# Differential attention on one NeuronCore: scores kept in SBUF by the maximum's pass and issued a step ahead, meta parts of four units turned beside the values' sums

## The chip, the cores and the metric

The kernel runs on one core of one Trainium2 chip. A core has five engines that run side by side, each through its own list of instructions in order, and that wait for one another by semaphores: TensorE (PE; its weight loads are listed apart as PEld), VectorE (DVE), ScalarE (ACT), GpSimd (POOL) and SyncE (SP, which only issues transfers here). The metric is the device time of one execution, in microseconds (us), as the median of several runs.

## The reference

The reference is one layer of an encoder over 1024 tokens and 16 learned meta tokens (width 1024): a projection, windowed attention (8 heads), differential attention (8 heads), an output projection, and a mixture of 32 experts, 4 for each token. What matters here is differential attention:

```python
scale = DIFF_DQ ** -0.5                       # DIFF_DQ = 32, DIFF_H = 8, DIFF_DV = 64
def one_block(qs):                            # 128 query rows at a time
    a, b = qs
    p1 = softmax(einsum('bqhd,bkhd->bhqk', a, k1) * scale)   # over 1024 + 16 keys
    p2 = softmax(einsum('bqhd,bkhd->bhqk', b, k2) * scale)
    return einsum('bhqk,bkhd->bqhd', (p1 - lam * p2), v)
```

So each head has two score matrices over the same keys, two softmaxes, and one product with the values. The head's output is normalised afterwards, per head, in the stage that follows.

## The kernel before

The kernel is a chain of stages, each a block of instructions for all engines with a barrier behind it: `project`, `attend_window`, `attend_diff`, `route` (output projection and routing), `experts`, `combine`. Only `attend_diff` is touched.

`attend_diff` goes through U = 64 units, a unit being one head h and one tile t of 128 query rows (unit n = 8h + t). Each engine's list is written out by hand over steps n = 0 to 71, a step doing different parts of several units:

- TensorE: `scores(n, i)` for i = 0, 1 gives the scores of half i of unit n, 128 rows by 1024 keys, into PSUM `s_ps[i]` (two banks, one buffer for each half). It waits until ScalarE has used the scores of the same half of unit n-1 (`s_used`). The queries' scores with the 16 meta keys are made for a whole head at once (`meta_scores`, 16 small products into `x_ps`). The combined weights of a unit are turned by eight transposes into `t_ps` (`transpose_part`, two groups of four) and a ninth, of the 16 meta columns, into `x_ps` (`transpose_meta`). `values` sums the product of values and turned weights for four units together (512 columns) in `o_ps[0:64]`: nine products, eight of 128 keys and one of the 16 meta keys. Two of the nine are issued in a step, in each fourth step three: one by itself between `scores(n, 0)` and the transposes, two after `scores(n, 1)`. Last, the sum of a group of four units is turned back by four small transposes into `x_ps` (L792).
- VectorE: `maximum(n, i)` is a `tensor_reduce` over the 1024 scores in PSUM (L640) and a 1-column minimum with the meta keys' part (L647). Then `invert` (reciprocal of the sums), `copy_meta` (the turned meta part, PSUM to SBUF, each unit), `combine_halves` (e0 + ratio x e1, 1040 columns, L662), and in some steps `store_out` (four scalings of 64 columns, L677) and `meta_scores` (two operations, each eighth step).
- ScalarE: for each half an exponential of the 1024 scores from PSUM (L600) and one of the 16 meta scores (L602), each followed by the read of its sum; between the two halves the two copies of the turned weights of unit n-2 (L587); in each fourth step the copy of the values' sum (L612).
- GpSimd: the sum of the two partial sums (L707) and the ratio (L711).

The order of the work in TensorE's list within step n is: `scores(n, 0)`, [one value product in each fourth step], the transposes of unit n-2, `scores(n, 1)`, two value products, [turning back], [`meta_scores`]. SP's list in this stage: the next stage's weights first, then the queries and keys of head h once all scores of head h-2 are made.

Of the kernel before, what the change touches and what calls it, by code (L numbers as in the profile page):

```python
# [22 lines left out]
ALU = mybir.AluOpType  # L23
ACT = mybir.ActivationFunctionType
AX = mybir.AxisListType
# [489 lines left out]
def attend_diff(nc, a, v_all, mixed, qk_dram, stacks, weights):  # L515
# [3 lines left out]
    with ExitStack() as ctx:  # L519
# [5 lines left out]
        e = sb("e", [P, 2, 2, KEYS])  # L525
        dsb = sb("dsb", [P, 2, KEYS])
# [3 lines left out]
        meta_s = sb("meta_s", [P, 2, 2 * NT, N_META])  # L530
        meta_nm = sb("meta_nm", [P, 2, 2 * NT])
        seq_nm = sb("seq_nm", [P, 4])
        nm = sb("nm", [P, 4])
        ls = sb("ls", [P, 2, 2, 2])
# [10 lines left out]
        scores_ready, max_ready, exp_done = sem("scores_ready"), sem("max_ready"), sem("exp_done")  # L545
        nm_ready, s_used = sem("nm_ready"), sem("scores_used")
        inverted = sem("inverted")
        total_done, ratio_done, combined = sem("total_done"), sem("ratio_done"), sem("combined")
        t_ready, t_copied = sem("p_transposed"), sem("pt_copied")
        x_ready, x_copied, meta_max = sem("x_ready"), sem("x_copied"), sem("meta_max")  # L550
        o_ready, ot_done = sem("o_ready"), sem("ot_copied")
        dve_chain = sem("dve_chain2")
# [3 lines left out]
        STEPS = U + 8  # L556
        block = ctx.enter_context(nc.Block())


        copied_in = lambda n: (n - 9) // 4 if n >= 9 and (n - 9) % 4 == 0 and (n - 9) // 4 < NG else None  # L560
        back_in = lambda n: copied_in(n - 1)

        order = [("scores", 0)]
        for n in range(STEPS):
            if 2 <= n <= U + 1:
                order.append(("meta", n - 2))
            if back_in(n) is not None:
                order.append(("back", back_in(n)))
            if n % NT == NT - 1 and n + 1 < U:
                order.append(("scores", (n + 1) // NT))  # L570
# [10 lines left out]
        def _(act):  # L581
            def copy_part(u, g):

                act.wait_ge(t_ready, 2 * u + g + 1)
                if g == 0 and u % 4 == 0 and u >= 8:
                    act.wait_ge(o_ready, u // 4 - 1)
                act.copy(pt[:, (u // 4) % 2, 4 * g:4 * g + 4, (u % 4) * P:(u % 4 + 1) * P],  # L587
                         t_ps[:, g, :].rearrange("p (c n) -> p c n", n=P)).then_inc(t_copied, 1)
# [3 lines left out]
            for n in range(STEPS):  # L592
                for i in range(2):
                    if n < U:
                        act.wait_ge(nm_ready, 2 * n + i + 1)
                        if n >= 2 and i == 0:
                            act.wait_ge(combined, n - 1)
                            act.wait_ge(total_done, n - 1)
                        k = (2 * n + i) % 4
                        act.activation(e[:, n % 2, i, 0:SEQ], S(i), ACT.Exp, bias=nm[:, k:k + 1],  # L600
                                       accum_out=ls[:, n % 2, 0, i:i + 1]).then_inc(s_used, 1)
                        act.activation(e[:, n % 2, i, SEQ:KEYS], meta_s[:, (n // NT) % 2, 2 * (n % NT) + i, :], ACT.Exp,  # L602
                                       bias=nm[:, k:k + 1], accum_out=ls[:, n % 2, 1, i:i + 1]).then_inc(exp_done, 1)
                    if i == 0 and 2 <= n <= U + 1:
                        copy_part(n - 2, 0)
                        copy_part(n - 2, 1)
                g = copied_in(n)
                if g is not None:
# [3 lines left out]
                    act.copy(ot[:, :], o_ps[0:DV, :]).then_inc(ot_done, 1)  # L612

        @block.vector
        def _(dve):
# [11 lines left out]
            def meta_scores(h):  # L627
                dve.wait_ge(x_ready, use_of[("scores", h)] + 1)
                if h >= 2:
                    dve.wait_ge(exp_done, 2 * NT * (h - 1))  # L630
# [1415 lines left out]
```

## Time and profile before

| | us |
|---|---|
| median of 3 runs (lowest to highest) | 2760.18 (2759.84 to 2764.11) |
| the profiled execution, its own time | 2772.98 |
| span of the profile | 2771.0 |
| `attend_diff` in it, from its first product to the next stage's first transfer | 478.5 to 820.7 |
| TensorE busy over the span | 2447.0 (88%) |
| VectorE busy | 1766.8 (64%) |
| ScalarE busy | 1435.9 (52%) |
| granted TensorE clock, mean over the span | 0.938 |

Times inside the profile are counted in us from the start of its span. The granted clock is a share of full speed, which is 2.4 GHz; the other level is 1.2 GHz. A group of instructions is named by its line of the kernel. An fp32 or fp32r product is recorded as several MATMUL rows: a value product is two of them, a half unit's scores two. Ends of matmuls are modelled; starts are not.

### The profile page before, as it was taken

How to read it: one execution, taken by the hardware profiler on the slowest of the kernel's cores; microseconds unless marked ns; L12 is line 12 of the kernel's file. 1: busy time of each engine (PE TensorE's matmuls, PEld its weight loads, DVE VectorE, ACT ScalarE, POOL GpSimd, SP SyncE). 2: the span in 40 equal slices, each digit the busy share in tenths (PEclk: the TensorE clock that was granted, in tenths of full speed). 3: DMA queues.
4: the chain of work that ended last, by engine and by line, in shares of the span. 5: the costliest groups of instructions: out<-in, count | busy, mean ns of one | idle time of the engine just before them, and what ended most of it. 6: DMA issues, size and time to landing. Idle time of an engine off the chain costs nothing. (4 is left out here: it accounts for less than half of the span.)

```text
span 2771.0 us, 33947 instructions
## 1 busy us (share of the span) xinstructions
PE 2447.0 (88%) x10437; PEld 1703.2 (61%) x10438; DVE 1766.8 (64%) x2143; ACT 1435.9 (52%) x1863; POOL 472.0 (17%) x539
## 2 busy tenths in 40 slices
PE   7999599899989928999999998999999999999950
PEld 3555265444435516777778776777777777777740
DVE  1444355899964446767675566666776667688654
ACT  1111154777751126675664565655665657577540
POOL 1443200111101221121211122111211111112110
PEclk9999799899999959999999999999999999999975
DMA  4221450232103347787785677776876669699767
GB/s 182 65 65 51 108 108 23 84 62 62 31 20 77 83 163 273 261 283 289 266 319 203 218 265 278 243 253 211 292 259 243 223 231 340 223 351 337 247 241 276
DMA packets 248412, 540.75 MB, mean 195 GB/s; under 512 B 27200, under 2 KB 58176, under 8 KB 246224
## 3 DMA queue, kind: packets, MB, share of 16 engines
q1 hardware_dynamic: 226304, 501.10, 53.8%
q0 software_dynamic: 20880, 34.49, 3.4%
q10 hardware_dynamic: 1152, 4.19, 0.4%
q8 instruction: 42, 0.69, 0.1%
q14 instruction: 34, 0.28, 0.0%
HBM read 513.63 MB, written 60.15 MB: 207 GB/s over the span
## 5 line engine op out<-in xcount | busy, mean ns | idle before, releaser
L1661 DVE TENSOR_TENSOR wlo<-raw,whi 128x2048 fp32r<-128x2048 f32 x387 | 881.6, 2291 | 360.6 <-ACT whi L1546 359.4
L1546 ACT CAST whi<-raw 128x2048 fp32r<-128x2048 f32 x387 | 737.5, 1913 | 275.7 <-PE gl_ps L1816 149.3
L1818 PE MATMUL gl_ps<-whi,xt_hi 128*128 128x512 f32 x1056 | 428.7, 406 | 64.1 <-ACTq L1609 40.9
L1819 PE MATMUL gl_ps<-wlo,xt_hi 128*128 128x512 f32 x1056 | 421.7, 399 | 0.0
L1820 PE MATMUL gl_ps<-whi,xt_lo 128*128 128x512 f32 x1056 | 420.1, 398 | 0.0
L1818 PEld LDWEIGHTS gl_ps<-whi,xt_hi 128*128 128x128 f32 x1056 | 204.5, 194 | 117.2 <-issue 68.7
L422 PE MATMUL pp<-w_in_sb,ut 128*128 128x512 f32 (+3 forms) x688 | 271.2, 552 | 0.8 <-issue 0.8
L1820 PEld LDWEIGHTS gl_ps<-whi,xt_lo 128*128 128x128 f32 x1056 | 204.4, 194 | 44.5
L1819 PEld LDWEIGHTS gl_ps<-wlo,xt_hi 128*128 128x128 f32 x1056 | 204.9, 194 | 41.8
L1482 POOL CAST sel<-onehot 128x128 fp32r (+1 forms) x66 | 48.2, 731 | 1017.6 <-PE gl_ps L1824 774.9
L1818 PE MATMUL y_ps<-whi,ht_hi 128*128 128x512 f32 x512 | 208.3, 407 | 0.0
L422 PEld LDWEIGHTS pp<-w_in_sb,ut 128*128 128x128 f32 (+1 forms) x688 | 125.4, 185 | 130.1 <-issue 125.0
L1820 PE MATMUL y_ps<-whi,ht_lo 128*128 128x512 f32 x512 | 202.0, 395 | 0.0
L1819 PE MATMUL y_ps<-wlo,ht_hi 128*128 128x512 f32 x512 | 201.7, 394 | 0.0
L600 ACT ACTIVATE e<-s_ps,nm 128x1024 f32<-128x1024 f32 x128 | 143.5, 1121 | 72.9 <-DVE nm L647 72.9
L1816 PE MATMUL gl_ps<-wlo,xt_hi 128*64 128x512 f32 x416 | 164.5, 395 | 0.0
L1815 PE MATMUL gl_ps<-whi,xt_hi 128*128 128x512 f32 x416 | 162.2, 390 | 0.0
L640 DVE TENSOR_REDUCE seq_nm<-s_ps 128x1 f32<-128x1024 f32 x128 | 155.7, 1217 | 9.6 <-PE s_ps L721 7.1
L763 PE MATMUL o_ps<-pt,v_all 128*64 128x512 f32 (+1 forms) x288 | 142.9, 611 | 0.8 <-ACT ot L612 0.8
L1477 POOL DMA_INDIRECT xg<-v_dram,idn x66 | 116.2, 1760 | 146.8 <-DMA idn<-slot_dram 115.3
L247 ACT COPY pr<-pp 128x512 f32<-128x512 f32 (+3 forms) x43 | 23.0, 540 | 185.5 <-PE pp L422 185.5
L1293 PE MATMUL o_ps<-w_out_sb,mt 128*128 128x512 f32 x256 | 116.7, 606 | 0.9 <-DVE mt L1173 0.9
(260 smaller groups left out, 3532.6 us busy)
## 6 DMA issues: line engine op xcount, KB each, us to landing
raw<-in_w_mlp SPq DMA_DIRECT2D x390, 1024.0 KB, 5.1
yk<-y_dram SPq DMA_DIRECT2D x8, 2048.0 KB, 7.8
w_in_sb<-in_w_in SPq DMA_DIRECT2D x8, 1152.0 KB, 14.2
k_st<-qk_dram SPq DMA_DIRECT2D x32, 260.0 KB, 7.5
xs<-in_x SPq DMA_DIRECT2D x16, 512.0 KB, 7.3
q_st<-qk_dram SPq DMA_DIRECT2D x32, 256.0 KB, 6.6
qk_dram<-qk_hi SPq DMA_DIRECT2D x8, 832.0 KB, 4.5
qk_dram<-qk_lo SPq DMA_DIRECT2D x8, 832.0 KB, 7.5
```

Of the source, the lines that this page charges most:

```text
L422: ins = pe.matmul(pp[0:r, n % 4, 0:c1 - c0], ut[:, t % 2, k, 0:r], w_sb[:, k, c0:c1], start=(k == 0), stop=(k == KC - 1))
L600: act.activation(e[:, n % 2, i, 0:SEQ], S(i), ACT.Exp, bias=nm[:, k:k + 1], accum_out=ls[:, n % 2, 0, i:i + 1]).then_inc(s_used, 1)
L640: dve.tensor_reduce(seq_nm[:, k:k + 1], S(i), AX.X, ALU.max, negate=True).then_inc(max_ready, 1)
L763: ins = pe.matmul(o_ps[0:DV, :], vt, pt[0:r, g % 2, c, :], start=(c == 0), stop=(c == 8))
L1293: ins = pe.matmul(o_ps[:, 2 * (t % 2) + b, :], mt[:, t % 2, k, :], w_sb[:, k, 512 * b:512 * b + 512], start=(k == 0), stop=(k == KC - 1))
L1546: act.copy(whi[:, k % SPL, :], raw[:, k % RAW, :]).then_inc(hi_done, 1)
L1661: dve.tensor_tensor(wlo[:, k % SPL, :], raw[:, k % RAW, :], whi[:, k % SPL, :].bitcast(F32), ALU.subtract).then_inc(lo_done, 1)
L1815: ins = pe.matmul(bank, xh[:, 1, kc, :], hi, start=start, stop=stop, skip_group_check=True)
L1816: ins = pe.matmul(bank[0:FEW], xh[:, 1, kc, 0:FEW], lo, start=False, stop=stop, skip_group_check=True)
L1818: pe.matmul(bank, xh[:, half, kc, :], hi, start=start, stop=False, skip_group_check=True)
L1819: pe.matmul(bank, xh[:, half, kc, :], lo, start=False, stop=False, skip_group_check=True)
L1820: return pe.matmul(bank, xl[:, half, kc, :], hi, start=False, stop=stop, skip_group_check=True)
```

## The change

Eight parts, all inside `attend_diff`:

1. The maximum's pass becomes a `tensor_tensor_reduce` that adds a tile of zeros to the scores, multiplies by -1, writes the negated scores (1024 columns) into `e` in SBUF, and takes the minimum, starting from the meta part. The separate 1-column minimum and its buffers go.
2. GpSimd places the 16 negated meta scores of both halves behind them in `e`; ScalarE then does one exponential in place over 1040 columns of SBUF (scale -1), whose sum goes straight to `total`. GpSimd's addition of partial sums goes.
3. `scores(n + 1, i)` is issued in step n and waits for the maximum's pass over unit n, half i (`nm_ready`) instead of ScalarE's exponential.
4. The turned meta part goes to `o_ps[0:16]`, four units side by side, while the values' sum goes to `o_ps[64:128]` of the same bank; ScalarE copies it once for four units (`copy_meta`), VectorE's copy for each unit goes.
5. The value products start a step later (LAG = 7) and stand at the head of TensorE's step; the ninth is issued in one row with two others.
6. ScalarE's copies of the turned weights are split around the second exponential.
7. `back`, `store_out` and `meta_scores` move to the front of the step, on VectorE in between `invert` and the second maximum; the meta scores of the next head are made two steps earlier.
8. STEPS is U + 9 instead of U + 8.

```diff
@@ scalar
+            def exponent(n, i):
+                act.wait_ge(nm_ready, 2 * n + i + 1)
+                act.wait_ge(meta_in, n + 1)
+                if n >= 16 and i == 0:
+                    act.wait_ge(ratio_done, n - 15)
+                k = (2 * n + i) % 4
+                act.activation(e[:, n % 2, i, :], e[:, n % 2, i, :], ACT.Exp, bias=nm[:, k:k + 1], scale=-1.0,
+                               accum_out=total[:, n % 16, i:i + 1]).then_inc(exp_done, 1)
+            def copy_meta(g):
+                act.wait_ge(m_ready, 4 * g + 4)
+                if g >= 2:
+                    act.wait_ge(o_ready, g - 1)
+                act.copy(pt[0:N_META, g % 2, 8, :], o_ps[0:N_META, :]).then_inc(m_copied, 1)
...
             for n in range(STEPS):
+                if n < U:
+                    exponent(n, 0)
+                g = weighed_in(n)
                 if g is not None:
                     act.wait_ge(o_ready, g + 1)
...
+                    act.copy(ot[:, :], o_ps[DV:P, :]).then_inc(ot_done, 1)
+                if 2 <= n <= U + 1:
+                    copy_first(n - 2)
+                if n < U:
+                    exponent(n, 1)
+                if 2 <= n <= U + 1:
+                    copy_second(n - 2)
+                    if (n - 2) % 4 == 3:
+                        copy_meta((n - 2) // 4)
@@ vector
             def maximum(n, i):
-                dve.tensor_reduce(seq_nm[:, k:k + 1], S(i), AX.X, ALU.max, negate=True).then_inc(max_ready, 1)
...
-                dve.tensor_tensor(nm[:, k:k + 1], seq_nm[:, k:k + 1], meta_nm[:, (n // NT) % 2, at:at + 1],
-                                  ALU.min).then_inc(nm_ready, 1)
...
+                    dve.wait_ge(exp_done, 2 * n + i - 3)
+                    dve.wait_ge(combined, n - 1)
+                dve.tensor_tensor_reduce(e[:, n % 2, i, 0:SEQ], S(i), zero[:, :], -1.0, meta_nm[:, (n // NT) % 2, at:at + 1],
+                                         ALU.add, ALU.min, nm[:, k:k + 1]).then_inc(nm_ready, 1)
...
                     maximum(n, 0)
                 if 1 <= n <= U:
                     invert(n - 1)
+                if back_in(n) is not None:
+                    store_out(back_in(n))
+                if scores_in(n) is not None:
+                    meta_scores(scores_in(n))
                 if n < U:
                     maximum(n, 1)
                 if 1 <= n <= U:
                     combine_halves(n - 1)
@@ gpsimd
+            for n in range(U + 1):
+                if n < U:
+                    h, at = n // NT, 2 * (n % NT)
+                    if n >= 2:
+                        pool.wait_ge(combined, n - 1)
+                    pool.wait_ge(x_copied, use_of[("scores", h)] + 1)
+                    pool.tensor_copy(e[:, n % 2, :, SEQ:KEYS], meta_s[:, h % 2, at:at + 2, :]).then_inc(meta_in, 1)
+                if n >= 1:
...
@@ tensor
             def scores(n, i):
...
-                    pe.wait_ge(s_used, 2 * n + i - 1)
+                    pe.wait_ge(nm_ready, 2 * n + i - 1)
...
+                pe.transpose(o_ps[0:N_META, (u % 4) * P:(u % 4 + 1) * P], dsb[:, u % 2, SEQ:KEYS], ident[:, :]
+                             ).then_inc(m_ready, 1)
...
+                    ins = pe.matmul(o_ps[DV:P, :], vt, pt[0:r, g % 2, c, :], start=(c == 0), stop=(c == 8),
+                                    skip_group_check=True)
...
             for n in range(STEPS):
+                if back_in(n) is not None:
+                    back(back_in(n))
+                if scores_in(n) is not None:
+                    meta_scores(scores_in(n))
+                if LAG <= n < U + LAG:
+                    q, i = divmod(n - LAG, 4)
+                    values(9 * q + 2 * i, 9 * q + 2 * i + (3 if i == 3 else 2))
+                if n + 1 < U:
+                    scores(n + 1, 0)
+                if 2 <= n <= U + 1:
+                    transposes(n - 2)
+                if n + 1 < U:
+                    scores(n + 1, 1)
```

## Rows read from the trace of the kernel before

**Rows 1.** Stretches: us; busy PE, PEld, DVE, ACT, POOL; granted clock; DMA share; GB/s.

```profile
478.40:518.60 40.20, 28.03 (x97) 17.71 (x98) 29.55 (x53) 25.58 (x67) 3.29 (x13) 0.66 0.37 129
...
558.60:798.40 239.80, 229.41 (x993) 112.07 (x991) 217.50 (x399) 190.25 (x494) 25.83 (x97) 1.00 0.21 45
798.40:820.70 22.30, 18.09 (x59) 6.28 (x58) 6.95 (x19) 7.04 (x16) 0.87 (x3) 1.00 0.00 1
```

**Rows 2.** TensorE in order of time, 640 to 702: start, us, what, idle before.

```profile
641.01 1.95 PE L736 MATMUL x_ps<-k_st,q_st 128*128 128x16 f32 x16
...
661.21 0.73 PE L721 MATMUL s_ps<-k_st,q_st 128*128 128x512 f32 x2
662.92 1.09 PE L744 MATMUL t_ps<-ident,dsb 128*128 128x128 f32 x8 [0.98 <-DVE dsb L662]
...
680.77 1.95 PE L736 MATMUL x_ps<-k_st,q_st 128*128 128x16 f32 x16
682.58 0.71 PE L721 MATMUL s_ps<-k_st,q_st 128*128 128x512 f32 x2
683.12 1.03 PE L744 MATMUL t_ps<-ident,dsb 128*128 128x128 f32 x8
...
684.02 0.72 PE L721 MATMUL s_ps<-k_st,q_st 128*128 128x512 f32 x2
684.67 1.93 PE L763 MATMUL o_ps<-pt,v_all 128*64 128x512 f32 x4
686.53 0.73 PE L721 MATMUL s_ps<-k_st,q_st 128*128 128x512 f32 x2
687.20 1.07 PE L763 MATMUL o_ps<-pt,v_all 128*64 128x512 f32 x2
688.20 1.09 PE L744 MATMUL t_ps<-ident,dsb 128*128 128x128 f32 x8
...
689.80 2.07 PE L763 MATMUL o_ps<-pt,v_all 128*64 128x512 f32 x4
691.80 0.73 PE L721 MATMUL s_ps<-k_st,q_st 128*128 128x512 f32 x2
692.83 1.09 PE L744 MATMUL t_ps<-ident,dsb 128*128 128x128 f32 x8 [0.29 <-DVE dsb L662]
...
696.69 0.73 PE L721 MATMUL s_ps<-k_st,q_st 128*128 128x512 f32 x2
697.46 1.09 PE L744 MATMUL t_ps<-ident,dsb 128*128 128x128 f32 x8
```

**Rows 3.** Groups by line in `attend_diff`: count, busy us, mean ns, idle before.

```profile
L640 DVE TENSOR_REDUCE seq_nm<-s_ps 128x1 f32<-128x1024 f32 x128 | 155.7, 1217 | 9.6 <-PE s_ps L721 7.1
L600 ACT ACTIVATE e<-s_ps,nm 128x1024 f32<-128x1024 f32 x128 | 143.5, 1121 | 72.9 <-DVE nm L647 72.9
...
L662 DVE SCALAR_TENSOR_TENSOR dsb<-e,ratio 128x1040 f32<-128x1040 f32 x64 | 83.3, 1302 | 5.3 <-POOL ratio L711 0.5 <-issue 0.4
```

**Rows 4.** The same view of the windowed attention before it, shapes apart.

```profile
L957 DVE CUSTOM_DVE_ANT_0 sm<-sa_ps,masks 128x400 f32<-128x400 f32 x48 | 24.8, 558 | 1.6 <-PE sa_ps L888 1.6
...
L957 DVE CUSTOM_DVE_ANT_0 sm<-sa_ps,masks 128x272 f32<-128x272 f32 x16 | 6.5, 432 | 21.5 <-PE sa_ps L888 21.5
```

**Rows 5.** VectorE in order of time: first half maxima of units 0 and 7.

```profile
482.29 1.23 DVE L640 TENSOR_REDUCE seq_nm<-s_ps 128x1 f32<-128x1024 f32 x1 [0.22 <-PE s_ps L721]
...
518.68 1.23 DVE L640 TENSOR_REDUCE seq_nm<-s_ps 128x1 f32<-128x1024 f32 x1 [0.47 <-PE s_ps L721]
```

**Rows 6.** TensorE in order of time in the same first steps.

```profile
496.18 1.79 PE L744 MATMUL t_ps<-ident,dsb 128*128 128x128 f32 x8 [2.37 <-DVE dsb L662]
...
497.83 2.17 PE L721 MATMUL s_ps<-k_st,q_st 128*128 128x512 f32 x4
```

**Rows 7.** The end of the stage, TensorE in order of time.

```profile
796.09 0.73 PE L721 MATMUL s_ps<-k_st,q_st 128*128 128x512 f32 x2
...
812.09 6.36 PE L763 MATMUL o_ps<-pt,v_all 128*64 128x512 f32 x14
```

More of the change, by code:

```diff
@@ L693, in _ @@
                     combine_halves(n - 1)
-                if back_in(n) is not None:
-                    store_out(back_in(n))
-                if n % NT == NT - 1 and n + 1 < U:
-                    meta_scores((n + 1) // NT)
         @block.gpsimd
@@ L701, in _ @@
             pool.wait_ge(lam_done, 1)
[L702 to L712 removed]
+            for n in range(U + 1):
[6 more added lines that the diff above has]
+                if n >= 1:
+                    u = n - 1
+                    pool.wait_ge(inverted, u + 1)
+                    if u >= 2:
+                        pool.wait_ge(combined, u - 1)
+                    pool.tensor_scalar(ratio[:, u % 2:u % 2 + 1], total[:, u % 16, 0:1], inverse[:, u % 16, 1:2], lw[:, 5:6],
+                                       ALU.mult, ALU.mult).then_inc(ratio_done, 1)
         @block.tensor
@@ L762, in values, with back @@
                     vt = v_all[0:r, c, 128 + h * DV:128 + (h + 1) * DV]
-                    ins = pe.matmul(o_ps[0:DV, :], vt, pt[0:r, g % 2, c, :], start=(c == 0), stop=(c == 8))
+                    ins = pe.matmul(o_ps[DV:P, :], vt, pt[0:r, g % 2, c, :], start=(c == 0), stop=(c == 8),
+                                    skip_group_check=True)
                     if c == 8:
                         ins.then_inc(o_ready, 1)
+            def back(g):
+                pe.wait_ge(ot_done, g + 1)
+                free_x(("back", g))
+                for j in range(4):
+                    ins = pe.transpose(x_ps[:, j * DV:(j + 1) * DV], ot[:, j * P:(j + 1) * P], ident[0:DV, 0:DV])
+                ins.then_inc(x_ready, 1)
@@ L767, in _ @@
             pe.wait_ge(const_landed, 16 * 5)
             meta_scores(0)
+            for i in range(2):
+                scores(0, i)
             for n in range(STEPS):
-                weighing = 6 <= n < U + 6
-                m = 9 * ((n - 6) // 4) + 2 * ((n - 6) % 4)
-                if n < U:
-                    scores(n, 0)
-                if weighing and (n - 6) % 4 == 3:
-                    values(m, m + 1)
-                    m += 1
-                if 2 <= n <= U + 1:
-                    pe.wait_ge(combined, n - 1)
-                    transpose_part(n - 2, 0)
-                    transpose_part(n - 2, 1)
-                    transpose_meta(n - 2)
@@ L783, in _ @@
-                if n < U:
-                    scores(n, 1)
-                if weighing:
-                    values(m, m + 2)
-                g = back_in(n)
-                if g is not None:
-                    pe.wait_ge(ot_done, g + 1)
-                    free_x(("back", g))
-                    for j in range(4):
-                        ins = pe.transpose(x_ps[:, j * DV:(j + 1) * DV], ot[:, j * P:(j + 1) * P], ident[0:DV, 0:DV])
-                    ins.then_inc(x_ready, 1)
-                if n % NT == NT - 1 and n + 1 < U:
-                    meta_scores((n + 1) // NT)
+                if back_in(n) is not None:
+                    back(back_in(n))
```

128 lines of the change are left out of this document (47 added, 81 removed).

## The prediction

> **What bounds the kernel now.** I began with the table of stages in the page: TensorE is busy 88% of the span, and the stage that the diff touches lies between 478.5 and 820.7. Everything outside it stays, so the question is what sets the pace of that stage's 342.2 us. I cut it into stretches [rows 1]. In the middle (six heads, 558.6 to 798.4) TensorE runs at full clock and is busy 229.4 of 239.8 us, VectorE 217.5, ScalarE 190.3; in the first 40 us everything is less busy and the granted clock is 0.66, a mixture of the two levels; in the last 22 us only TensorE works.
>
> Busy time alone doesn't say who waits, so next I read TensorE's list in order of time [rows 2]. The reader is to take the distances between starts, since ends are modelled. One cycle of eight steps has the same sequence again: from 641.01 to 680.77 the meta scores of a head come back after 39.76 us, 4.97 us a step. Within it, scores to transposes is 0.54 where nothing is awaited (682.58 to 683.12), but 1.71 at 661.21, 1.03 at 691.80 and 0.77 at 696.69. In each of these the transposes wait for VectorE's combined weights. By eight steps, the excess over 0.54 is once 1.17, twice 0.49, twice 0.23: 2.6 us. The row's own idle figure for such a wait (0.29 at 692.83 against an excess of 0.49) is smaller, because the end of the product before is modelled late. So TensorE does 39.76 - 2.6 = 37.2 us of work in eight steps and loses 2.6 to VectorE. VectorE is the second engine at the limit: two maxima at 1.22, one combination at 1.30 [rows 3], and behind them the small operations that wait for each other.
>
> **VectorE's part.** Removed in each step: two `tensor_reduce` of 1.217 [rows 3], two 1-column minima with the wait between maximum and minimum, and the copy of the turned meta part. Added: two `tensor_tensor_reduce` over 1024 columns from PSUM with one input in SBUF. This form is in the trace at 400 and 272 columns: 558 and 432 ns [rows 4], 0.98 ns a column, so 0.558 + 624 x 0.00098 = 1.17 us; at the 1.19 ns a column that the whole of L640 comes to, 0.558 + 0.74 = 1.30. I take 1.2. A step of VectorE is then 2 x 1.2 + 1.30 + about 0.16 for the reciprocal + 0.2 (the four scalings of each fourth step) + 0.1 (meta scores of each eighth) = 4.2 us as durations, which overlap a little. That is 0.4 below TensorE's work for a step (below). The waits that held it back go too: it need not wait for its own 1-column result, and scores stand ready a step ahead.
>
> **ScalarE and GpSimd.** The exponential is 1.12 from PSUM over 1024 columns [rows 3]; now it is one of 1040 columns in SBUF, and the second small one with its accumulator read is gone. At worst it costs what the pair costs now. With two copies of the turned weights, the sum's copy and the new copy of the meta part once in four steps, ScalarE stays below its present 190.3/48 = 4.0 us a step, below TensorE: nothing on the path. GpSimd's placement of 2 x 16 columns runs beside VectorE's first maximum, 1.2 us long; without that cover it would delay an exponential by a few tenths.
>
> **TensorE's part.** The same products and transposes are issued. What changes is their order: the single value product (scores to value 0.67, value to transposes 1.00) joins two others in a row. In a row a product costs half of 1.86 at most (684.67 to 686.53 is two), and 6.36 us for seven in the tail [rows 7] gives 0.91. So 1.67 turns into 0.54 + 0.91, 0.22 less, twice in eight steps. Work of eight steps: 37.2 - 0.4 = 36.7 with the roundings, that is 4.58 a step. The value products write other partitions of the bank; in this trace L763 and the window's value product write only the lower ones, so a cost of the upper ones isn't shown. I take nothing, since the streamed columns (512) and the loaded ones (64) are the same; the upper bound is the 0.14 that 16-row weights add (689.80 to 691.80 is 2.00 against 1.86), 2.25 times a step, 18 us in all.
>
> Do any waits of TensorE remain? Step n of TensorE, starting at P, is now: two value products to P+1.86, `scores(n+1, 0)` to 2.4, transposes of unit n-2 to 3.35, `scores(n+1, 1)` to 4.0 (4.6 with its share of the rest). The first group of turned weights is there at P+2.95; ScalarE copies it (0.55) and then does the second exponential, ready at P+4.9. VectorE inverts at P+5.0, GpSimd's ratio follows at P+5.5, VectorE's second maximum ends by P+6.3 and the combination at P+7.6. The transposes of unit n come at P+2 x 4.6+2.4 = P+11.6: 4 us to spare. The scores' waits are for maxima ending at about P+0.6 (needed at P+1.86) and P+1.7 (needed at P+3.35). With the four scalings or the meta scores (0.8 each) in front of the second maximum it is P+2.6 or P+4.0, against P+3.7 and P+5.2: still in time. Behind VectorE's new wait (the reciprocal for ScalarE's second exponential, which itself is now behind a copy) stand the second maximum and with it `scores(n+1, 1)`; this is the tightest loop, with about 1 us left in it. Head loads are issued seven steps before use and land in time.
>
> So steps 7 to 62 cost 56 x (4.97 - 4.58) = 22 us less.
>
> **The first steps.** Units 0 to 7 begin 36.4 us apart in sum [rows 5], 5.2 each, though no values are summed before step 6. Here VectorE and TensorE wait for each other in turn and TensorE's half clock makes it dear: eight transposes and the ninth take 1.65 and four score products 2.17 [rows 6], with 2.37 us of idle time before. In the new order the scores are there before VectorE wants them. Step 0 takes 2 maxima, 2.5 us; step 1 3.8 (it adds a combination); from step 2 the longer of VectorE's 3.9 (no scalings yet) and TensorE's 3.9 to 4.1 at the low clock, say 4.1. Step 7 begins at 2.5 + 3.8 + 5 x 4.1 = 26.8 instead of 36.4: 9.6 less. It may be less by what the low clock costs in the first value products, which now also come at that clock; I take 8.5. Bounds: 3 (only the score waits go) and 10.
>
> **The end.** After the last scores 16 value products and two turns stand in TensorE's list now, 18 and three in the new one, but the waits for the last combinations, in which TensorE now has nothing else to do, go. From the start of step 63 (796.09 [rows 7]) to 820.7 it is 24.6 us now, and 3 x 2.9 + 2.8 + 0.8 + 0.4 + 9 x 0.9 + 2.4 = 23.2 after. 1.4 less; bounds 0 and 3.
>
> **Sum.** 22 + 8.5 + 1.4 = 32 us in the stage. A stage is rarely as tight as its list: where a semaphore arrives late by a tenth in each step it gives back 0.5 to 2 us; I take 1.5 off: **30.5 us**. The profiled execution took 2772.98 (span 2771.0 and 2 around it), 12.8 above the median of the runs; the stages outside hold that difference as well before as after, so the profile should read about 2740 and the median 2760.2 - 30.5 = **2729.7**.
>
> A rule and this trace: the Trainium skill ("Trainium Kernel Development and Optimization", Performance Expectations) calls the matmul row's busy time a bad metric, since matmuls are pipelined, and names the weight load's busy share instead. By that share, 112.1 of 239.8 us or 47% [rows 1], TensorE would be far from its limit, and the stage could fall to VectorE's 4.2 a step, 25 us more than I forecast. The trace agrees with the first half (the modelled ends hide half of the waits) but not with the second: fourteen rows of value products that had all been ready take 6.36 us in the tail [rows 7], 0.45 each, and the same 0.46 to 0.48 in the middle of a step, with the weight port idle between them.
>
> **Rivals.**
> *Only the shown idle time goes.* If TensorE's busy time is real, there are 239.8 - 229.4 = 10.4 us to gain in 48 steps, 12 in 56, with 3 to 6 at the start and 1 at the end: 17.5 less, 2742.7. Against it: the 0.54 and 1.03 of the same pair of starts. Chance 0.17 (any cause that leaves half the gain, a slower upper half of the bank too).
> *TensorE is not the limit after all.* VectorE's 4.2 a step: 25 us more, 2705. Nothing shows value products closer than 0.45 a row. Chance 0.03.
> *VectorE's new pass is slow (the other side).* If `tensor_tensor_reduce` with its 1024-column write into SBUF takes two passes, 2.4 us, a step costs 1.8 + 4.8 = 6.6 and the stage 64 x 1.6 = 104 us more, 2864. It decides from (4.97 - 1.8)/2 = 1.6 us a pass on. For it: the form is shown only up to 400 columns and its starting value was a constant there. Against it: 0.98 ns a column between 272 and 400. Chance 0.04.
> *The loop closes.* Copy, second exponential, reciprocal, second maximum, scores: were that loop 5 us, the steps stay as they are and only start and end gain, or not even that: within 0.2%. Chance 0.03.
>
> **How the numbers follow.** Likeliest: 0.73, its own range 2722 to 2737. The range that leaves out 0.2 reaches into the first rival: 2722 to 2744. Within 0.2% (5.5 us, about what this kernel's runs can tell from no change): 0.03; slower 0.05, faster 0.92.
>
> **What would show it.** In the changed profile: the new pass at 1.15 to 1.3 us; meta scores coming back after 36.5 to 37 us; scores to transposes 0.54 in all steps but the first; no idle time of the transposes behind the combination in the middle; VectorE idle before its reciprocal; unit 7's first maximum 27 to 29 us after unit 0's; stage end near 789. Wrong it would be if value products in the upper partitions took more than 0.47 us a row, if the pass took over 1.6, or if the middle stretch showed TensorE waiting for `nm`.

## The result, and the profile after

| | before | after |
|---|---|---|
| median, runs side by side (lowest to highest) | 2762.14 (2759.84 to 2764.99, 4 runs) | 2716.97 (2715.16 to 2722.54, 4 runs) |
| the profiled execution, its own time | 2772.98 | 2722.54 |
| the stage: from its first meta scores to the next stage's first VectorE pass over data (L1160 before, L1165 after) | 342.9 | 308.9 |
| behind it, to the end of the span (2771.0 and 2720.7) | 1949.6 | 1936.5 |

The ratio is 0.9838 (95% interval 0.9815 to 0.9862), 45 us less where 30.5 were predicted, and below the range's lower end of 2722. A second set of runs, later, gives 2716.7 against 2756.5, ratio 0.9852 (0.9826 to 0.9879), 41 us by the ratio. The stage's 34 us are close to what was forecast (32, less 1.5 for late semaphores). The rest, 7 to 11 us, lies behind it.

Stretches of the changed kernel, columns as in [rows 1]:

```profile
475.30:508.20 32.90, 26.24 (x109) 18.86 (x109) 29.14 (x52) 22.39 (x40) 3.67 (x14) 0.71 0.44 158
508.20:762.10 253.90, 253.90 (x1137) 134.36 (x1136) 230.12 (x408) 207.27 (x366) 31.21 (x113) 1.00 0.24 51
520.00:760.00 240.00, 240.00 (x1081) 127.52 (x1080) 218.09 (x383) 196.12 (x347) 29.21 (x106) 1.00 0.21 45
762.10:783.60 21.50, 19.00 (x68) 7.26 (x67) 5.18 (x13) 6.22 (x13) 0.34 (x1) 1.00 0.00 0
```

In the middle TensorE is now busy in 240.00 of 240.00 us (229.4 of 239.8 in [rows 1]), and it is the only engine without a gap. The change takes 3.50 us out of its cycle of eight steps. Its list in order of time, one cycle of eight steps from one meta score group to the next:

```profile
642.09 1.85 PE L741 MATMUL x_ps<-k_st,q_st 128*128 128x16 f32 x16
643.87 1.93 PE L771 MATMUL o_ps<-pt,v_all 128*64 128x512 f32 x4
645.73 0.73 PE L726 MATMUL s_ps<-k_st,q_st 128*128 128x512 f32 x2
646.30 1.03 PE L751 MATMUL t_ps<-ident,dsb 128*128 128x128 f32 x8
...
647.20 0.72 PE L726 MATMUL s_ps<-k_st,q_st 128*128 128x512 f32 x2
647.85 2.93 PE L771 MATMUL o_ps<-pt,v_all 128*64 128x512 f32 x6
650.71 0.73 PE L726 MATMUL s_ps<-k_st,q_st 128*128 128x512 f32 x2
...
678.35 1.85 PE L741 MATMUL x_ps<-k_st,q_st 128*128 128x16 f32 x16
```

The row at 678.35 is the next head's meta scores. The cycle is 678.35 - 642.09 = 36.26 us, 4.53 a step (4.97 in [rows 2], 4.58 forecast). Scores to transposes is 0.57 (645.73 to 646.30), with no idle time in brackets (a bracket at the end of a row gives the engine's idle time before it, and what ended it); two value products cost 1.86, three in a row 2.86.

The stage's groups by line (out<-in, count, busy us, mean ns, idle before), which answer to [rows 3]:

```profile
L658 DVE CUSTOM_DVE_ANT_0 e<-s_ps,zero,meta_nm 128x1024 f32<-128x1024 f32 x128 | 163.5, 1278 | 11.5 <-DVE dsb L673 9.2 <-PE s_ps L726 1.8 <-ACT e L586 0.3
L586 ACT ACTIVATE e<-e,nm 128x1040 f32<-128x1040 f32 x128 | 149.1, 1165 | 9.7 <-DVE nm L658 8.6
```

The new pass lasts 1278 ns. ScalarE's idle time before its exponential fell from 72.9 us to 9.7: the maxima now come in time. VectorE in order of time, both maxima of unit 0 and the first of unit 7, against [rows 5]:

```profile
479.94 1.28 DVE L658 CUSTOM_DVE_ANT_0 e<-s_ps,zero,meta_nm 128x1024 f32<-128x1024 f32 x1 [0.23 <-PE s_ps L726]
481.15 0.08 DVE L658 DVE_READ_ACCUMULATOR2_ANT nm<- 128x1 f32 x1
481.15 1.28 DVE L658 CUSTOM_DVE_ANT_0 e<-s_ps,zero,meta_nm 128x1024 f32<-128x1024 f32 x1
...
507.12 1.28 DVE L658 CUSTOM_DVE_ANT_0 e<-s_ps,zero,meta_nm 128x1024 f32<-128x1024 f32 x1 [0.17 <-DVE dsb L673]
```

Two passes in a row start 1.21 us apart (479.94, 481.15): 1.2 forecast. Unit 7 begins 27.2 us after unit 0, 36.4 before. The end, TensorE in order of time, against [rows 7]:

```profile
772.85 0.46 PE L780 MATMUL x_ps<-ident,ot 64*128 64x64 f32 x4 [0.67 <-ACT ot L617]
773.24 8.08 PE L771 MATMUL o_ps<-pt,v_all 128*64 128x512 f32 x18
781.99 0.46 PE L780 MATMUL x_ps<-ident,ot 64*128 64x64 f32 x4 [0.67 <-ACT ot L617]
```

Eighteen rows of value products into the upper partitions take 8.08 us, 0.449 each; [rows 7] has 0.454 for the lower ones (6.36 us for 14 rows). The upper half costs nothing.

### The profile page after: what moved, and what is told of

It reads as the page before. It is cut to its first block and busy times, and to the rows that moved or that the text cites. A ratio compares the mean times of both kernels' runs of the same rounds, so it can differ in the third digit from the quotient of the medians.

```text
span 2720.7 us, 33591 instructions
## 1 busy us (share of the span) xinstructions
PE 2430.1 (89%) x10437; PEld 1706.7 (63%) x10438; DVE 1741.3 (64%) x2080; ACT 1417.5 (52%) x1623; POOL 477.3 (18%) x539
## 5 line engine op out<-in xcount | busy, mean ns | idle before, releaser
L658 DVE CUSTOM_DVE_ANT_0 e<-s_ps,zero,meta_nm 128x1024 f32<-128x1024 f32 x128 | 163.5, 1278 | 11.5 <-DVE dsb L673 9.2
L586 ACT ACTIVATE e<-e,nm 128x1040 f32<-128x1040 f32 x128 | 149.1, 1165 | 9.7 <-DVE nm L658 8.6
L1482 POOL DMA_INDIRECT xg<-v_dram,idn x66 | 122.0, 1848 | 141.8 <-DMA idn<-slot_dram 112.1
```

The source lines that it names most:

```text
L586: act.activation(e[:, n % 2, i, :], e[:, n % 2, i, :], ACT.Exp, bias=nm[:, k:k + 1], scale=-1.0, accum_out=total[:, n % 16, i:i + 1]).then ...
L658: dve.tensor_tensor_reduce(e[:, n % 2, i, 0:SEQ], S(i), zero[:, :], -1.0, meta_nm[:, (n // NT) % 2, at:at + 1], ALU.add, ALU.min, nm[:, k: ...
L1482: pool.indirect_dma_start(out=xg[:, half, :], out_offset=None, in_=v_dram[:, :], in_offset=bass.IndirectOffsetOnAxis(ap=idn[:, half, 1:2], ...
```

## The experiments

My theory was that the stage's gain is TensorE's list without its waits, and that nothing outside moves. The open points were: how near VectorE is, which part of the change carries the gain, and where the 7 to 11 us outside the stage come from. "The stage" below is always the measure of the table's third row.

### How the two kernels repeat

The kernel before and the changed one once more.

> The kernel before, once more, to see how much of its profile repeats. Theory A (outside the changed stage the time depends on which short falls of TensorE's clock happen in the experts' stage, and these differ from execution to execution): the differential stage takes 342 us again within 0.5, but the experts' jobs 2 and 14, which took 51.9 and 45.1 us against 38.6 and 38.4 in the changed kernel, don't both repeat, and the experts' stage comes out anywhere between 1620 and 1636 us. Theory B (the changed kernel's experts' stage is faster because of where its code or its work lies in time): the stage repeats at 1635 us, the two long jobs with it.

> The changed kernel once more beside the kernel before, in more executions. In the profiles so far the changed stage gives 34 us and everything behind the stage takes 1926 to 1950 us in either kernel, from execution to execution. Theory A (the part of the first difference above 34 us was that scatter): the medians lie 34 to 41 us apart, and the stage in the profile takes 308.3 us within 0.5. Theory B (the changed kernel gains outside the stage as well): 43 us or more apart.

before_again: 2749.66, stage 342.1, behind it 1930.1. after_again: 2716.7 (2711.15 to 2722.26, 6 runs), ratio 0.9852; stage 308.0, behind it 1932.5. So in these two pairs the stage repeats within 1 us (a later execution of the kernel before took 344.7), and the part behind it does not: 1949.6 and 1930.1 in two executions of the kernel before. The prediction had read this part from one execution and carried it over.

### The changed kernel with its later stages at the time of before

Between `attend_diff` and `route`, ScalarE copies a tile of 1024 columns 28 times, each copy waiting for the one before; the stages behind start 32.4 us later.

```diff
+                delay(nc, 28)        # a block of its own: act.copy(t[:, :], t[:, :]), 28 times in a chain
                 route(...)
```

> The changed kernel with a stage of 28 copies on ScalarE, chained, between the differential stage and the output projection, some 34 us in which nothing else happens. Theory A: the experts' stage stays as in the changed kernel, between 1620 and 1630 us, and the total is 2717 + 34 = 2751 us, about 11 below the kernel before. Theory B in its form that the start of the experts' stage in time decides: the long jobs come back and the total is within 3 us of the kernel before, 2762.

2752.04 (10 runs), ratio 0.9972 (0.9949 to 0.9995). Without the 32.4 of the delay that is 2719.6, 2.7 above the changed kernel's first median, where a part behind the stage that hangs on its starting time would have brought some 8 back. The interval is 6 us to either side, so this speaks against the starting time and doesn't rule out a part of it.

### How near VectorE is

VectorE clears 640 columns of a spare tile in each step (592 ns, mean of 64), behind its reciprocal.

```diff
                 if 1 <= n <= U:
                     invert(n - 1)
+                if n < U:
+                    dve.memset(spare[:, :], 0.0)
```

> The changed kernel with a memset of 640 columns added to each of VectorE's steps behind the reciprocal, about 0.6 us a step, which is used for nothing. If TensorE alone sets the pace and VectorE has the 0.4 us a step and the loop the 1 us that the prediction gave them, most of it is hidden: 0 to 0.2 us a step, total 2717 to 2730. Rival, that VectorE is as close to the limit as TensorE: 64 x 0.6 = 38 us more, 2755.

2737.83 (5 runs), ratio 0.9918 (0.9885 to 0.9951); the stage 329.5, 21 more, 0.33 a step. Of 0.59 us put in, 0.26 disappear and 0.33 stand in the step. TensorE's list shows where, in a row that has no idle time in the changed kernel:

```profile
649.54 0.74 PE L729 MATMUL s_ps<-k_st,q_st 128*128 128x512 f32 x2 [0.21 <-DVE nm L659]
```

The second half's scores wait for the pass. So at this place of VectorE's list the slack is about 0.26 us a step, not the 0.4 of the prediction, and an operation longer than that would be paid for.

### Taking the issue ahead away

scores_late issues `scores(n, i)` in step n again; all else is the changed kernel.

```diff
-            for i in range(2):
-                scores(0, i)
...
-                if n + 1 < U:
-                    scores(n + 1, 0)
+                if n < U:
+                    scores(n, 0)
```

> The changed kernel with the scores of unit n issued in step n, as before, instead of a step ahead; all else stays. If the prediction's account of the steady steps is right (TensorE was held by VectorE, and the step ahead takes the wait of VectorE for fresh scores away), VectorE's first maximum of a step waits for the scores behind two value products, and the loop value products, scores, maximum, second maximum, combination, transposes of the next step closes: a step of 4.9 to 5.4 us instead of 4.53, total 2740 to 2770. Rival: the lighter work of VectorE and ScalarE alone gives the gain, the step ahead nothing: total within 4 us of 2717.

2778.38 (10 runs), ratio 1.0057 (1.0033 to 1.0082): slower than before, and above the 2770 that was the most expected. The stage takes 367.8, 59 more than in the changed kernel. Two of the waits from 540 to 800 us (engine, line, waited for: us, times, longest):

```profile
ACT e L586 <- DVE nm L658: 82.5, 66, 3.8
DVE e L658 <- PE s_ps L726: 59.6, 48, 3.9
```

And one of these 48, of the kind that comes once in four steps, in order of time:

```profile
642.14 0.58 ACT L617 COPY ot<-o_ps 64x512 f32<-64x512 f32 x1
...
642.78 0.46 PE L780 MATMUL x_ps<-ident,ot 64*128 64x64 f32 x4 [1.82 <-ACT ot L617]
...
643.17 1.93 PE L771 MATMUL o_ps<-pt,v_all 128*64 128x512 f32 x4
...
645.03 0.73 PE L726 MATMUL s_ps<-k_st,q_st 128*128 128x512 f32 x2
...
645.80 1.28 DVE L658 CUSTOM_DVE_ANT_0 e<-s_ps,zero,meta_nm 128x1024 f32<-128x1024 f32 x1 [2.30 <-PE s_ps L726]
```

TensorE's turning back waits 1.82 for a copy that ScalarE does behind an exponential; the value products follow, then the scores, and VectorE stands for 2.30. In the changed kernel the turning back has no wait in the middle stretch, where TensorE is never idle.

scores_late_tail also puts turning back, its scalings and the meta scores at the end of the step again, as before.

> The changed kernel with the scores of unit n in step n, and turning back, the four scalings and the meta scores at the end of the step, where they stood before. What is left of the change against the kernel before: the kept scores, one exponential for a half, GpSimd's placement, the meta parts by fours, the row of three value products, the split copies. If the step ahead is what lifts TensorE's waits, this lands near the kernel before: 4.8 to 5.1 us a step, 2750 to 2770 us. Rival: the lighter VectorE (4.2 instead of 4.6 a step) does it, and only the combination of late scores with the work at the front of the step made scores_late slow: 4.55 to 4.7 us a step, 2720 to 2735 us.

2769.33 (10 runs), ratio 1.003 (1.001 to 1.005), stage 359.9. Only 8 of the 59 us come from those places.

pass_alone goes the whole way: the new pass, one exponential and the turned meta parts, in the order of the kernel before on every engine (the value products still start a step later).

```diff
+                if n < U:
+                    scores(n, 0)
+                if weighing and i == 3:
+                    values(m, m + 1)
+                    m += 1
                 if 2 <= n <= U + 1:
                     transposes(n - 2)
+                if n < U:
+                    scores(n, 1)
+                if weighing:
+                    values(m, m + 2)
```

(ScalarE: both copies of turned weights between the exponentials, the sum's copy last.)

> The changed kernel's new pass, one exponential and turned meta parts, in the order of the kernel before: scores(n, i) in step n, the value products behind the scores of the second half, both copies of the turned weights between the exponentials, the sum's copy last. Theory: the pass that frees the score buffer early is worth nothing without issue ahead, and the order of the kernel before suits late scores better than that of the changed one (360 and 368 us); the stage takes 335 to 348, the time is within 0.3% of before. Rival 1 (the lighter VectorE does gain by itself, what made the two kernels with late scores slow was only the place of the value products and of the sum's copy): 320 to 330, 2740 to 2750. Rival 2 (late scores cost their 60 us wherever the rest stands): 355 or more, 2770.

The stage takes 336.8, 6 less than before: the lighter work alone gives about a sixth of the gain, and the theory's number for the stage (335 to 348) holds. TensorE's waits are back, for copies of ScalarE:

```profile
650.49 1.06 PE L751 MATMUL t_ps<-ident,dsb 128*128 128x128 f32 x8 [0.16 <-ACT pt L593]
...
652.73 1.90 PE L771 MATMUL o_ps<-pt,v_all 128*64 128x512 f32 x4 [0.60 <-ACT ot L625]
```

Yet its time is 2741.65 (6 runs), ratio 0.9936 (0.9915 to 0.9958), 18 us less by the ratio, where the theory had the time within 0.3% of before. Twelve of these are not in the stage (below).

### The issue ahead alone

ahead_alone is the kernel before with `scores(n + 1, i)` in step n, still waiting for ScalarE's exponential (`s_used`); the meta scores of the next head are made two steps earlier, as in the changed kernel.

```diff
-                if n < U:
-                    scores(n, 0)
+                if n + 1 < U:
+                    scores(n + 1, 0)
```

> The kernel before, with one thing of the change alone: scores(n + 1, i) issued in step n, waiting as before for ScalarE's exponential of unit n (and the meta scores of the next head made two steps earlier). Theory (the two halves of the change need each other: a score buffer that comes free only behind the exponential is too late for issue a step ahead): TensorE now waits in each step for the second exponential before its scores of the second half and has the two value products behind that wait; VectorE gets its scores no earlier than now. The stage stays within 6 us of its 342, the time within 0.3% of before. Rival (the order alone does most of it): the stage falls to 320 or less, 2738 or less.

3149.45 (4 runs), ratio 1.1423 (1.1386 to 1.146); the stage takes 727, twice as long. Both of my theories were far off. Two rows of its trace:

```profile
645.08 0.28 DVE L669 COPY pt<-x_ps 16x128 f32<-16x128 f32 x1 [4.30 <-PE x_ps L749]
...
648.05 0.73 PE L721 MATMUL s_ps<-k_st,q_st 128*128 128x512 f32 x2 [3.01 <-ACT e L600]
```

TensorE stands at the scores of the next unit until ScalarE has done with this one; behind these scores stand the transposes; for the ninth of them waits VectorE's copy of the turned meta part, which stands between its two maxima. ahead_copy_last moves that copy behind the second maximum, to tell which wait closes the loop.

> The kernel before with scores issued a step ahead (ahead_alone) and VectorE's copy of the turned meta part moved behind its second maximum. Theory (the copy between the two maxima closed the loop of ahead_alone): most of the 385 us go, the stage takes 335 to 365, 2755 to 2785. Rival (it is the release by the exponential that makes issue ahead so dear, TensorE stands before both halves' scores for ScalarE in each step): the stage stays above 500, 2900 or more.

3017.0 (4 runs), ratio 1.0948 (1.0928 to 1.0969); the stage 596. Moving the copy takes away 131 of the 384 us, and 253 are left: my theory fell here, the rival holds. Three of its waits from 540 to 800, the first two of them TensorE's for the exponential:

```profile
PEld s_ps L721 <- ACT e L600: 110.8, 50, 3.7
PE s_ps L721 <- ACT e L600: 89.4, 42, 3.6
DVE pt L669 <- PE x_ps L749: 85.5, 28, 3.7
```

In the same stretch TensorE is busy 170.6 of 260 us and has a mean granted clock of 0.80, so its products last longer too; how much of the 253 us is the clock, no run separates.

The four ways side by side, stage in us:

| | scores in their own step | a step ahead |
|---|---|---|
| exponential frees the score buffer | 342.9 (before) | 727, 596 |
| the pass into SBUF frees it | 336.8, 359.9, 367.8 | 308.9 (after) |

Neither half is worth much alone; one is ruinous alone. The four corners differ in the order of the work as well (parts 5 to 7 of the change): with late scores the old order takes 336.8 and the new one 359.9 or 367.8. No run has the new pass and the issue ahead in the old order, so what the new order adds to the 34 us isn't shown, apart from the two details that follow.

### Two details of the order

values_split issues the ninth value product by itself between scores and transposes; copies_together puts both copies of turned weights between the two exponentials.

```diff
-                    values(9 * q + 2 * i, 9 * q + 2 * i + (3 if i == 3 else 2))
+                    values(9 * q + 2 * i, 9 * q + 2 * i + 2)
                 if n + 1 < U:
                     scores(n + 1, 0)
+                if LAG <= n < U + LAG and i == 3:
+                    values(9 * q + 8, 9 * q + 9)
```

> The changed kernel with the ninth value product of four units again by itself, between the scores and the transposes. The prediction put the row of three at 0.22 us less, once in four steps; the starts of the changed profile make it (2.86 + 0.57) against (1.86 + 0.67 + 1.00). So the head scores come back after 36.26 + 0.2 to 0.6 us, the stage takes 2 to 5 us more, the total stays within 5 of the changed kernel. Rival: the single product between the scores and the transposes costs more than its place, since it moves the transposes and with them the second exponential later: 10 us or more.

> The changed kernel with both copies of the turned weights again between the two exponentials on ScalarE. By the prediction's working this puts 0.55 us more into the loop (first group of transposes, copy, second exponential, reciprocal, second maximum, scores) that had about 1 us left: nothing or up to 0.1 us a step, total within 5 us of the changed kernel. Rival: the loop has less room than that, VectorE waits for the exponential before its reciprocal and TensorE behind it: 0.3 us a step or more, 20 us.

values_split: 2722.96 (4 runs), ratio 0.9882 (0.9845 to 0.9919), stage 311.1; its eight steps take 36.56, 0.30 more than the changed kernel's, where the prediction counted 0.44. copies_together: 2724.96 (4 runs), ratio 0.9867 (0.9831 to 0.9904), stage 312.3. Each is a matter of 2 to 4 us in the stage (308.9 and 308.0 in the changed kernel). The medians lie 6 and 8 us above the changed kernel's beside them, a little more than the 5 that were expected, but the intervals of both overlap its interval.

### Where the rest of the gain lies

The kernel before twice more, for the part behind the stage.

> The kernel before once more, one look, for the part behind the stage. Theory (that part differs from execution to execution in either kernel, 1926 to 1950 us in ten profiles): 1928 to 1950, the stage 341.5 to 343. Rival (it is longer in the kernel before than in the changed one by the 8 us that the stage's gain leaves open): 1938 or more.

> As before_b, a third look at the kernel before: the same two theories. If one of the two has five or more instruction packets beside a wait of TensorE in the second job of the experts, the scatter of 14 us in its times is this wait.

Times 2761.65 and 2763.2, stages 342.1 and 344.7, behind them 1941.6 and 1939.1. TensorE in order of time at the same place of before, before_b and before_c, the second job of the experts (the part of the experts' stage that works on one block of tokens), one block of rows for each:

```profile
1086.62 0.79 PE L1818 MATMUL gl_ps<-whi,xt_hi 128*128 128x512 f32 x1 [13.38 <-issue]
1087.20 0.63 PE L1819 MATMUL gl_ps<-wlo,xt_hi 128*128 128x512 f32 x1
```

```profile
1068.84 0.61 PE L1824 MATMUL y_ps<-b2t,sel 128*128 128x512 f32 x2
1081.66 0.79 PE L1818 MATMUL gl_ps<-whi,xt_hi 128*128 128x512 f32 x1 [12.21 <-issue]
```

```profile
1072.83 0.61 PE L1824 MATMUL y_ps<-b2t,sel 128*128 128x512 f32 x2
1085.52 0.79 PE L1818 MATMUL gl_ps<-whi,xt_hi 128*128 128x512 f32 x1 [12.07 <-issue]
```

TensorE stops for 12 to 13 us on no semaphore that the profile shows, and the products after it last 0.63 and not 0.39: the clock has fallen to 1.2 GHz (granted 0.50 from 1086.6 to 1090). The transfer queues of these three whole spans have five more packets of instructions, of 16 KB each, than before_again and after:

```profile
q8 instruction: 42, 0.69, 0.1%
```

```profile
q8 instruction: 37, 0.61, 0.1%
```

Four of the five fall into the stretch of the wait, as the view of before from 1072 to 1088 shows; before_again, which begins its second job at 1070.6 without a stop, has none from 1060 to 1088:

```profile
q8 instruction: 4, 0.07, 2.1%
```

The same goes together at the first job: in all 19 profiles of this study TensorE waits 9.2 to 10.9 us before its first products, and three or four such packets fall into that wait. So the trace points to TensorE waiting for its own code to be fetched. It doesn't say whose instructions a packet holds, and no run changes the fetching alone, so this is a reading and isn't shown.

Of the 19 profiles, in all kernels, four have this wait in the second job: three of the four of before, and ahead_copy_last. Behind the stage they take 1939.1 to 1951.0, mean 1945; the fifteen others 1925.8 to 1942.2, mean 1934. If three in four executions of before have it, it is worth three quarters of 11.6 us, 8.7: an estimate from four profiles, and about the part of the gain that the stage leaves open.

Does it hang on where the later code lies? The next four add 32 or 64 small turns (64 by 64) to TensorE's list in steps 0 and 1 of the stage, and so shift all that follows.

```diff
+                if n < 2:
+                    for _ in range(k // 2):        # k = 32 or 64
+                        pe.transpose(o_ps[0:DV, 0:DV], ident[0:DV, 0:DV], ident[0:DV, 0:DV])
```

> The kernel before with 32 small turns (64 by 64, into the sum's free bank) added to TensorE's list in steps 0 and 1 of the stage, where it mostly waits; they shift all later code by 64 rows. Theory (the 12 us wait in the second job of the experts hangs on how TensorE's code lies): it goes, 37 instruction packets, and the time falls by 4 to 8 us net of at most 2 us for the added work, 2752 to 2757. Rival (the wait comes by chance in this program): as in before, 2758 to 2763, the part behind the stage near 1940.

> The same with 64 small turns, 3 to 5 us in the stage. Theory: another position of the code, so the wait may be there or not, but then in its profile and its times alike: 1930 to 1934 behind the stage without it, 1938 or more with it. Rival (chance): 2760 to 2768.

> The changed kernel with the same 32 small turns, one look. Theory (the layout decides): the 12 us wait can appear here, which no profile of the changed kernel has; then 1938 or more behind the stage and 42 packets. Rival (it belongs to the stage before it): none, 1930 to 1938 as before it.

> The changed kernel with 64 small turns, one look: as after_pad32, a second position of the code. Either 37 packets and no such wait, or 42 packets and a wait of about 12 us.

| | time (runs) | stage | behind it | instruction packets |
|---|---|---|---|---|
| before_pad32 | 2755.58 (10) | 345.4 | 1930.0 | 39 |
| before_pad64 | 2766.42 (10) | 346.4 | 1936.1 | 43 |
| after_pad32 | 2722.74 (1) | 309.1 | 1936.3 | 39 |
| after_pad64 | 2722.57 (1) | 312.2 | 1933.4 | 43 |

None of the four has the wait in the second job. But both programs with 64 turns have one in a later job. There TensorE stops for 4.5 to 4.6 us in each of the other 17 profiles, and for 10 us in these two (9.98 and 10.01), again with three packets of instructions in it and the products behind it at 1.2 GHz. before_pad64, the rows and then the packets from 1596 to 1607:

```profile
1596.16 0.62 PE L1827 MATMUL gl_ps<-b2t,sel 128*64 128x512 f32 x2
1606.77 0.79 PE L1821 MATMUL gl_ps<-whi,xt_hi 128*128 128x512 f32 x1 [9.98 <-DVE wlo L1664]
1607.35 0.63 PE L1822 MATMUL gl_ps<-wlo,xt_hi 128*128 128x512 f32 x1
```

```profile
q8 instruction: 3, 0.05, 2.6%
```

The row names VectorE's pass as what ended the wait, but the same pass comes after TensorE's start in before_pad32 (1603.02 against 1599.98), so TensorE doesn't need it there. So the six profiles with 42 or 43 packets are the six with such an added wait, and the thirteen with 37 or 39 have none. Moving the code by 64 turns moved the wait to another job, in both kernels alike; this speaks for the place of the code having a part in it. It can't be the whole of it, since before and before_again are the same kernel, one with the wait and one without.

The times agree only loosely. before_pad32 has 2.5 us more in the stage than the mean of the four profiles of before and yet a median 6.4 below the 2761.97 of before beside it, as it should be without the wait, but its ratio of 0.9986 (0.9969 to 1.0004; 19 runs of before) can't be told from no change. before_pad64 is 4.5 us slower (1.0019, 1.0005 to 1.0033), with 3.5 more in the stage; one wait gone and the other 5.5 us longer should have left it near before. What makes the second job's wait come in one execution of the kernel before and not in another stays open.

## Why the prediction was right in the stage and wrong in its number

**What bounds the stage: right.** TensorE's list sets the pace, the distances between starts told its real work, and about half of what VectorE held back was hidden in modelled ends (10.4 us shown idle in the 48 steps of the middle, and 19 us of waits gone from as many steps). The first rival (only the shown idle time goes, 17.5 us) is refuted by 34; the second (VectorE at 4.2 a step, 2705) by the steps at 4.53 with TensorE busy in all of them. The weight port in the full stretch is busy 127.52 of 240 us, 53%. The Trainium skill ("Trainium Kernel Development and Optimization", Performance Expectations) names MFU (the share of the peak arithmetic rate) and the weight load's busy share as the good metrics; only the second was weighed in the prediction. By it TensorE would still have half its time free; here it has none.

**The steady steps: right, a little low.** 56 x (4.97 - 4.58) = 22 became 56 x (4.97 - 4.53) = 24.6. Eight steps gave 3.50 us where 3.04 were counted. The ninth product's share is 0.30 of them (0.44 counted), so the waits were 3.2 and not 2.6: 0.6 us of waits had been taken for work. The pass (1.2 forecast, starts 1.21 apart) and the upper partitions (nothing) were right.

**VectorE's slack: a little high.** 0.26 us a step by dve_more, against 0.4. It decided nothing, but the changed kernel is that near to its next limit.

**The first steps: right.** 9.2 us of the 9.6 worked out, 8.5 taken. The kernel before varies here (units 0 to 7 begin 36.4, 34.4, 34.4 and 37.3 us apart in its four profiles), the changed one less (27.2 twice).

**The end: a little high.** From TensorE's start of step 63 to the end of the stage it is 25.3 us before and 24.4 after, 0.9 less where 1.4 were forecast. Two of the three turns back wait 0.67 each for their copy, which the sum had in part left out.

**The parts together: in part luck.** By TensorE's starts of steps 0, 7 and 63 the stage's 34 us are 9.9 in the first seven steps, 26.5 in the next 56 and 0.9 at the end, less 3.4 before step 0, where the scores of unit 0 now stand (before_again and after_again: 7.7, 27.2 and 0.9, less 1.7). The sum had 22 for the 56 steps and nothing for the time before step 0; these two misses cancel in part.

**The 1.5 taken off for late semaphores: not there.** No run shows this term. With the issue a step ahead no wait of TensorE is left in the middle into which a late tenth could fall.

**"The stages outside hold that difference as well before as after": the step that failed.** It took the part outside the stage for one number that both kernels share. It is a distribution: 1930.1 to 1949.6 behind the stage in four profiles of the same kernel before. The execution that I read had the 13.38 us wait of the second job, and so had the two later ones near the median; the changed kernel's two have none. The sum for the median held 30.5 for the stage and 0 for the rest; the runs show 34 and 7 to 11. The changed profile was to read about 2740 by this step and reads 2722.5. The wait stood in the trace of before, in a stage that I left unread because the diff doesn't touch it. Had I read it, its going could have been a case with a time, at most 12 us less, 2718. That the wait accounts for the 7 to 11 us rests on four profiles of the kernel before; whether the changed kernel loses it by the place of its code or otherwise is not settled.

**What the change gains it by.** I had argued part by part, as if the gains added up. The table of four ways shows a product: the lighter VectorE alone gives 6 us, the issue ahead alone costs 250 and more, both (with the new order of the work) give 34.

## What to carry to other kernels

Issue an engine's work a step ahead only together with an early release of the buffer that it fills: in an ordered list a wait at the head holds back everything behind it, and what stands behind it may be what the releaser waits for. Where an engine in order is the limit, read distances between starts in a cycle that repeats; here the idle figures beside modelled ends showed about half of the wait. And before a small difference is predicted for a whole program, look through the stages that the change leaves alone for a single long wait on nothing, and for packets of instructions that fall into it: it may not be there in the next execution.

## What the runs showed of the hardware

- `tensor_tensor_reduce` over 128 x 1024 fp32, one input in PSUM, one in SBUF, output in SBUF: 1278 ns, starts 1.21 us apart in a row, and 0.08 us for the read of its minimum that overlaps the next instruction. The plain maximum over the same scores takes 1217 ns in [rows 3], so the copy into SBUF cost 61 ns at most.
- The exponential in place over 1040 columns in SBUF takes 1165 ns, 44 more than over 1024 from PSUM [rows 3].
- A wait of TensorE of 12 to 13 us on no semaphore shown, once in an execution, in four of 19 profiles, and one of 10 us in place of 4.5 in two more; three or four 16 KB packets of instructions fall into each, and the next products are at the 1.2 GHz level (0.63 us a row and not 0.39).
- A stage in which TensorE keeps waiting can also lose clock: ahead_alone's granted clock is 0.76 from 540 to 760 us, ahead_copy_last's 0.80 from 540 to 800, where before and after have 1.00 from 540 to 760.
